# Loads issued a stage early, a third value buffer in GLA, its last head's end among its outputs, and a wait for constants moved, in a decoder layer on one Trainium2 core

## The reference

```python
mod = silu(c) @ w_ada + b_ada                      # shift1, scale1, gate1, shift2, scale2, gate2
h   = rmsnorm(x) * (1 + scale1) + shift1
p   = h @ w_in                                     # one projection for GLA, RWKV-7 and the two gates
# GLA, 4 heads: q, k of width 128, v and output gate of width 256, low-rank decay gate (rank 16)
la  = log_sigmoid(p_a @ w_gla_gate + b) / 16       # p_a: 16 columns of p, "gaT" in the kernel
per chunk of 64 tokens, with b = cumsum(la):
    o = (q exp(b)) S + tril((q exp(b)) (k exp(-b))^T) v
    S = exp(b_last) S + (k exp(b_last - b))^T v
og  = o * rsqrt(mean(o^2) + eps) * g * silu(gg)    # per head
# RWKV-7, 16 heads of 64: token shift, decay from a low-rank tanh, delta-rule state, group norm, gate
merged = sigmoid(g1) * (og @ w_b_gla) + sigmoid(g2) * (o_r @ w_b_rw)
x   = x + gate1 * rmsnorm(merged @ w_out)
# PEER: 8 heads, top-16 of 128 x 128 single-neuron experts, then gelu and a weighted sum
x   = x + gate2 * rmsnorm(peer(rmsnorm(x) * (1 + scale2) + shift2))
```

## Time and profile before

| | us |
|---|---|
| median of 3 runs | 5053.77 (5053.18 to 5062.45) |
| the profiled execution | 5051.28 |
| its span, first to last instruction | 5049.4 |
| mean granted TensorE clock | 0.922 |

### The profile page before, as it was taken

One profiled execution on the slowest core, in us unless ns is written; L12 is line 12 of the kernel. 1 busy time (PEld: TensorE's weight loads), 2 busy tenths in 40 slices (PEclk: granted clock), 3 DMA queues, 4 the chain that ended last, 5 costly groups with the idle time before them and its releaser, 6 DMA issues. The chain is left out here.

```text
span 5049.4 us, 80491 instructions
## 1 busy us (share of the span) xinstructions
PE 4346.1 (86%) x30920; PEld 2976.9 (59%) x30920; DVE 3328.2 (66%) x6528; ACT 1124.7 (22%) x2258; POOL 1677.7 (33%) x1412
## 2 busy tenths in 40 slices
PE   6999997875888887997988759999989899989970
PEld 6999996654777775653978634443434344434430
DVE  4232322445666661112997749999999999999998
ACT  2000001334555552124233320111100101111101
POOL 0000000001212210000143446666666566666666
PEclk9999998577999998998999879999999999999985
DMA  5422223211011014114022269999999999999987
GB/s 209 168 96 93 93 93 122 79 62 63 26 42 32 26 30 170 73 51 159 26 84 86 77 214 393 374 386 341 384 352 402 334 400 356 387 345 389 370 336 296
DMA packets 350603, 1012.43 MB, mean 201 GB/s; under 512 B 39116, under 2 KB 123020, under 8 KB 344760
## 3 DMA queue, kind: packets, MB, share of 16 engines
q0 software_dynamic: 156672, 570.49, 29.0%
q1 hardware_dynamic: 193592, 437.38, 23.9%
HBM read 903.76 MB, written 103.99 MB: 200 GB/s over the span
## 5 line engine op out<-in xcount | busy, mean ns | idle before, releaser
L2778 PE MATMUL peer_v_b<-peer_vt,peer_mix 128*128 128x512 f32 x2048 | 943.1, 615 | 123.8 <-DVE peer_mix L2615 80.0
L2766 PE MATMUL peer_s_b<-dense_hT_d,peer_ut 128*128 128x512 f32 x2048 | 901.0, 593 | 38.3 <-DMA peer_G2s<-mod 38.3
L2550 POOL DMA_INDIRECT peer_ring<-in_peer_v,peer_idx x544 | 712.6, 1310 | 290.1 <-issue 160.6
L2778 PEld LDWEIGHTS peer_v_b<-peer_vt,peer_mix 128*128 128x128 f32 x2048 | 402.0, 198 | 649.2 <-issue 495.9
L2544 POOL DMA_INDIRECT peer_ring<-in_peer_u,peer_idx x544 | 596.6, 1097 | 477.7 <-DVE peer_acc L2667 231.0
L2766 PEld LDWEIGHTS peer_s_b<-dense_hT_d,peer_ut 128*128 128x128 f32 x2048 | 389.7, 190 | 529.0 <-issue 490.4
L1524 POOL TENSOR_TENSOR rw_An<-rw_abT,rw_join 128x256 f32<-128x256 f32 x160 | 134.5, 847 | 1650.5 <-DVE rw_abT L1437 1316.2
L2667 DVE SCALAR_TENSOR_TENSOR peer_acc<-peer_ring,peer_coef,peer_acc 128x1024 f32<-128x1024 f32 x534 | 653.7, 1279 | 0.0
L2704 DVE CUSTOM_DVE_ANT_0 peer_ring<-peer_ring,peer_h 128x1024 f32<-128x1024 f32 x544 | 637.5, 1220 | 2.0 <-DVE peer_h L2681 1.0
L57 PE MATMUL proj_acc<-proj_hT_high,proj_w_low 128*128 128x352 f32 x1584 | 513.8, 324 | 16.7 <-DVEq L401 16.7
L58 PE MATMUL proj_acc<-proj_hT_low,proj_w_high 128*128 128x352 f32 x1584 | 508.6, 321 | 0.0
(11 more groups left out here) (424 smaller groups left out, 6531.6 us busy)
## 6 DMA issues: line engine op xcount, KB each, us to landing
peer_ut<-in_peer_ut SPq DMA_DIRECT2D x128, 512.0 KB, 8.1
peer_vt<-in_peer_v SPq DMA_DIRECT2D x128, 512.0 KB, 8.9
pT<-proj_o SPq DMA_DIRECT2D x66, 528.0 KB, 2.9
front_w<-in_w_in SPq DMA_DIRECT2D x66, 512.0 KB, 3.7
G<-route_G SPq DMA_DIRECT2D x32, 1024.0 KB, 9.3
peer_gt<-G SPq DMA_DIRECT2D x64, 512.0 KB, 7.2
proj_w_ada<-in_w_ada SPq DMA_DIRECT2D x16, 1024.0 KB, 6.1
peer_ring<-in_peer_u,peer_idx POOLq DMA_INDIRECT x544, 11.9
```

What stands on the lines that cost most here:

```text
L2550: pool.indirect_dma_start(out=ring[:, k, :], out_offset=None, in_=t["peer_v"], in_offset=bass.IndirectOffsetOnAxis(ap=idx[U % 2][:, k:k + ...
L2766: last = pe.matmul(s_b[:, n % 3, :], ut[:, n % UT, k, :], hT_d[:, k, :], start=(k == 0), stop=(k == KD - 1))
L2778: last = pe.matmul(v_b[:, m % 4, :], mix[:, part % 2, e, tokens], vt[:, part % 2, e, cols], start=(e == 0), stop=(e == PART - 1))
```

## The change

- `projection` takes a `GlaAhead` and an `RwkvConsts`. GlaAhead holds a room of 6 x M per partition, gaT, wz, cst and starts. The room's first part is the ring of `w_ada`, now of 3 chunks. Before the last two stores of pT, SP waits for the last chunk's use and for 13 stores of each buffer, and issues 9 loads for GLA (wz, cst, starts, q and k of head 0, values and gates of head 0) and the 13 constants of RWKV. The gate columns are copied straight into GLA's `gaT`; its DRAM tensor is gone, and the stores of `mod` no longer follow its store.
- `gla` has three value buffers (the first is the room's). `load_vg(2)` is issued after head 0's scaling, and in the loop the values of head h + 2 instead of h + 1.
- The last head follows a list of its own, in which its end (`l`) stands among its own turns, samples and outputs. GLA_ORDER serves the first three heads.
- `rwkv` finds its constants loaded. It puts its low-rank tiles into `bE` and `kE`, so the first pair's tiles are loaded at once, and stores the shift of the low-rank columns behind them. At pair 1 SP issues the loads of `MergeAhead`: ogT and both weights of the branches.
- `merge` loads only orT itself. Its two branches are two tiles, and the second block takes the first one's room.
- `peer_experts`: VectorE waits for `iota_in` at first and for `consts_in` only where tile 0 is finished; TensorE's wait for the constants is gone.
- `build` nests the stages so that what is shared lives long enough; this adds three clean-ups, one behind gla and two behind merge.

```diff
-def projection(nc, t, xT, modT, sg, w, w_in, wg, wg_in):
-    CHUNKS, RING, FIRST = 2 * KD, 4, 2
+def projection(nc, t, xT, modT, sg, w, w_in, wg, wg_in, ahead, consts):
+    CHUNKS, RING, FIRST = 2 * KD, 3, 2
-        wa = s.sb("w_ada", [P, RING, QUAD])
+        wa = ahead.room[:, :, :].rearrange("p a m -> p (a m)")[:, 0:RING * QUAD].rearrange("p (r c) -> p r c", r=RING)
-        og = s.sb("og", [16, M])
+        og = ahead.gaT
...
+                sp.wait_ge(wa_used, CHUNKS)
+                for n in range(W):
+                    sp.wait_ge(stored[n], 16 * (6 * GH // W + 1))
+                ahead.load(sp, t)
+                consts.load(sp, t)
                 for n in range(W):
                     sp.wait_ge(first_out, (ITER - 1) * W + n + 1)
                     sp.wait_ge(rest_out, (ITER - 1) * W + n + 1)
                     sp.dma_start(t["pT"][PT - W + n], o[:, n, :]).then_inc(stored[n], 16)
-                sp.wait_ge(first_out, PT + 1)
-                sp.wait_ge(rest_out, PT + 1)
-                sp.dma_start(t["gaT"], og[:, :]).then_inc(stored[0], 16)
...
 GLA_ORDER = (
     "eptepxspeetpopxxetespoxtsxepesoeteoxseptoxxpptsoepxtspxxoesppo",
 )
+GLA_LAST = (
+    "texeselllteoexexeteseoexetesexsotolxlstoxxtsoxtsxxolslollllll",
+)
...
-    for h in range(GH):
+    for h in range(GH - 1):
...
-    return steps + end(GH - 1)
+    return steps + last_head(GH - 1)
...
+class GlaAhead(Stage):
+    def load(self, sp, t):
+        sp.dma_start(self.wz[:, :, :], t["w_gate"].rearrange("h r p -> r h p")).then_inc(self.first_in, 16)
+        sp.dma_start(self.cst[:, :, :], t["gla_cst"].rearrange("h p n -> p h n")).then_inc(self.first_in, 16)
+        sp.dma_start(self.starts[:, :], t["starts"][:, 0:M].broadcast_to([P, M])).then_inc(self.first_in, 16)
+        for n in range(2):
+            sp.dma_start(self.room[:, n, :], t["pT"][n * GH]).then_inc(self.qk_in, 16)
+        for n in range(4):
+            sp.dma_start(self.room[:, 2 + n, :], t["pT"][2 * GH * (1 + n // 2) + n % 2]).then_inc(self.vg_in, 16)
...
-        vg = [s.sb(f"vg{n}", [P, 4, M]) for n in range(2)]
+        vg = [ahead.room[:, 2:6, :]] + [s.sb(f"vg{n}", [P, 4, M])[:, :, :] for n in (1, 2)]
...
                 sp.wait_ge(scaled, 3)
                 load_qk(1)
+                load_vg(2)
...
-                        if h + 1 < GH:
-                            load_vg(h + 1)
+                        if h + 2 < GH:
+                            load_vg(h + 2)
...
+class RwkvConsts(Stage):
+    def load(self, sp, t):
+        for name, shape in self.SHAPES.items():
+            dst = self.tiles[name]
+            src = t[name].broadcast_to([P, MW]) if name == "starts" else t[name]
+            sp.dma_start(dst[:, :, :] if len(shape) == 3 else dst[:, :], src).then_inc(self.consts_in, 16)
+class MergeAhead(Stage):
+    def load(self, sp, t):
+        sp.dma_start(self.gla[:, :, :].rearrange("p (h a) m -> p h a m", a=2),
+                     t["ogT"].rearrange("h p a m -> p h a m")).then_inc(self.gla_in, 16)
+        for n in range(2):
+            sp.dma_start(self.w[:, n, :, :, :], t["w_br"][n]).then_inc(self.w_in[n], 16)
...
                 for n in range(2):
-                    sp.dma_start(raw[n], t["pT"][RW0 + 24 + n]).then_inc(consts_in, 16)
-                sp.wait_ge(sho_ready, 1)
-                sp.dma_start(t["new_shift_wg"].rearrange("n p b -> p n b"), sho[:, 0:2, :]).then_inc(shift_stored, 16)
-                sp.wait_ge(wa_ready, 1)
-                sp.wait_ge(cleared, CLEARED)
+                    sp.dma_start(raw_wg[n], t["pT"][RW0 + 24 + n]).then_inc(consts_in, 16)
...
+                    if j == 1:
+                        ahead.load(sp, t)
...
-                sp.dma_start(r_.iota[:, :], t["iota"].broadcast_to([P, TOP])).then_inc(consts_in, 16)
+                sp.dma_start(r_.iota[:, :], t["iota"].broadcast_to([P, TOP])).then_inc(iota_in, 16)
...
-                dve.wait_ge(consts_in, 16 * CONSTS)
+                dve.wait_ge(iota_in, 16)
...
+                    if tile == 0:
+                        dve.wait_ge(consts_in, 16 * CONSTS)
...
-                pe.wait_ge(consts_in, 16 * CONSTS)
...
-    for stage in (front, gla, rwkv, merge, peer):
-        with nc.cleanup_on_exit():
-            stage(nc, t)
+    with nc.cleanup_on_exit(), ExitStack() as ctx:
+        consts = RwkvConsts(nc, ctx)
+        with nc.cleanup_on_exit(), ExitStack() as ctx1:
+            ahead = GlaAhead(nc, ctx1)
+            with nc.cleanup_on_exit():
+                front(nc, t, ahead, consts)
+            with nc.cleanup_on_exit():
+                gla(nc, t, ahead)
+        with nc.cleanup_on_exit(), ExitStack() as ctx2:
+            ahead = MergeAhead(nc, ctx2)
+            with nc.cleanup_on_exit():
+                rwkv(nc, t, consts, ahead)
+            with nc.cleanup_on_exit():
+                merge(nc, t, ahead)
+    with nc.cleanup_on_exit():
+        peer(nc, t)
```

More of the change, by code:

```diff
@@ L480, in _, with front @@
                 project(0, wg2, 16)
-def front(nc, t):
+def front(nc, t, ahead, consts):
     with ExitStack() as ctx:
@@ L500, in front @@
             modulation(nc, t, xT, modT, sg, first)
-        projection(nc, t, xT, modT, sg, w, w_in, wg, wg_in)
+        projection(nc, t, xT, modT, sg, w, w_in, wg, wg_in, ahead, consts)
 GH, GV, GC = 4, 256, 64
@@ L535, in gla_steps, with last_head @@
     relative = lambda which, h: [(kind, head - h, x) for kind, head, x in stream(which, h)]
+    def last_head(h):
+        streams = {which: iter(stream(which, h)) for which in "tsoxe"}
+        streams["l"] = iter(end(h))
+        return [next(streams[which]) for which in "".join(GLA_LAST)]
     whole = {which: iter(relative(which, 1)) for which in "tsoxpe"}
@@ L552, in gla @@
         seq_rows = s.sb("seq_rows", [NS, NB])
[L553 to L557, removed]
-        vg = [s.sb(f"vg{n}", [P, 4, M]) for n in range(2)]
+        starts, gaT, wz, cst = ahead.starts, ahead.gaT, ahead.wz, ahead.cst
+        qk = ahead.room[:, 0:2, :]
+        vg = [ahead.room[:, 2:6, :]] + [s.sb(f"vg{n}", [P, 4, M])[:, :, :] for n in (1, 2)]
         S_in = s.sb("S_in", [P, NB, GV])
@@ L1035, in rwkv @@
+def rwkv(nc, t, consts, ahead):
     with ExitStack() as ctx:
         s = Stage(nc, ctx, "rw")
-        ident = s.sb("ident", [P, RH])
-        strict = s.sb("strict", [P, 2, RC])
-        incl = s.sb("incl", [P, 2, RC])
-        first_l = s.sb("first_l", [P, RC])
-        first_u = s.sb("first_u", [P, RC])
-        join = s.sb("join", [P, LEVELS, RC])
-        seq_rows = s.sb("seq_rows", [P, NB])
-        starts = s.sb("starts", [P, MW])
-        heads = s.sb("heads", [P, P])
-        mean = s.sb("mean", [P, P])
@@ L1047, in rwkv @@
-        cst = s.sb("cst", [P, PAIRS, 10])
+        ident, strict, incl, first_l, first_u, join, seq_rows, starts, heads, mean, cst, mu_wg, sh_wg = (
+            consts.tiles[name] for name in consts.SHAPES)
         keep_k, keep_x = s.sb("keep_k", [P, PAIRS]), s.sb("keep_x", [P, PAIRS, 3])
-        mu_wg, sh_wg = s.sb("mu_wg", [P, 2]), s.sb("sh_wg", [P, 2, NB])
         sh = s.sb("sh", [P, 3, NB])
@@ L1246, in _ @@
                 for n in range(2):
-                    last = act.copy(sho[:, n, :], raw[n][:, SEQ - 1:M:NT])
+                    last = act.copy(sho[:, n, :], raw_wg[n][:, SEQ - 1:M:NT])
                 last.then_inc(sho_ready, 1)
@@ L1709, with merge @@
 MP = (TILES + 1) * P
-def merge(nc, t):
+def merge(nc, t, ahead):
     with ExitStack() as ctx:
         s = Stage(nc, ctx, "mg")
-        br = s.sb("br", [P, 2, KD, M])
+        br = [ahead.gla, s.sb("rw", [P, KD, M])]
         mT = s.sb("mT", [P, KD, M])
-        w = s.sb("w", [P, 2, 2, KD, P])
+        w = ahead.w
         gt = s.sb("gt", [P, 2, M])
@@ L2807, in scratch @@
 def scratch(nc, t):
-    for name, shape in {"mod": [NSEQ, 6, D], "pT": [66, P, M], "gaT": [16, M],
+    for name, shape in {"mod": [NSEQ, 6, D], "pT": [66, P, M],
                         "ogT": [GH, P, 2, M], "orT": [PAIRS, P, M],
```

108 lines of the change are left out of this document (54 added, 54 removed).

## The result

The changed kernel takes 4993.43 us (median of 4 runs, 4987.22 to 4997.36), against 5054.03 for the kernel before: a ratio of 0.989 with a 95% interval of 0.9876 to 0.9904, that is 48 to 63 us less. I had forecast 4980, a gain of 71.6 us; it came to about 60, with the time inside the range (4961 to 4998). On a second chip it took 4986.68 against 5049.31 (ratio 0.9878, 0.9862 to 0.9895). The profiled execution is the one of 4993.53 us, with a span of 4991.7.

What follows compares the result with a forecast made beforehand. Five stages run in sequence with no single bound; TensorE's waits at six places were to shrink. Gains of 9.9, 22.5, 2.0, 11.3, 15.1 and 13.2, less 2.4, make 71.6 us off 5051.3: forecast 4980, range 4961 to 4998 (8 in 10).

Steps and rivals of the forecast that it cites:

- term 3: GLA's last head, its end placed among its outputs: -11.3 us at the end, +9 inside the head, net -2 (ends -11, +5).
- rival B: Expert stage: saturated, it takes its gain of 13 us back, so an earlier start only queues; 4993 us, chance 0.13.
- Term 1: Projection to GLA: with loads ahead and gaT on chip, GLA starts at 848.5 instead of 858.4, -9.9 us.
- rival F: Projection: w_ada's ring of three lands chunks late and TensorE waits, up to +79 us, 5059, slower than before; chance 0.03.
- Term 2: GLA, heads 2 and 3: a third value buffer removes both stalls at the first transpose, -10.96 and -11.50, together -22.5 us.
- Rival E: GLA, heads 2 and 3: the stall is not the value load, or its load comes late; +22.5, 5002 us, chance 0.04.
- rival D: GLA's last head: its new order costs all that was bounded, net +5 us instead of -2; 4987 us, chance 0.10.
- Term 4: GLA to RWKV: constants loaded a stage early bring the scan to 22.1 us after RWKV's first instruction, from 33.4; -11.3 us.
- Term 5: RWKV to merge: operands loaded ahead in pair 1 let TensorE start at 1966.0 instead of 1981.11; -15.1 us.
- Term 6: Router to experts: TensorE starts when its first weights land, 2974.0, not at the last constant; -13.2 us (ends 0, -17).
- Term 7: Stage ends: one more clean-up behind GLA, two at merge's, at 0.8 us each; +2.4 us (ends 1 and 4).
- rival C: GLA: without the stalls, heads 2 and 3 begin at TensorE's full clock; 4965 us, chance 0.10.

## Why the prediction was right or wrong

The step that failed is term 3, the price of the last head's new order inside the head: +9 us forecast, +25.1 measured, so that the last head lost 12.5 us where a gain of 2 was forecast. The measured 4993 is also the price that I had put on rival B, whose mechanism did not occur, and it lies in the range only because B set its upper end; term 3 at its own worst (+5) gives 4987. That the range held is luck.

**Term 1, right.** 848.5 forecast, 847.91 measured. The ring of three cost nothing: rival F falls by the projection's unchanged waits.

**Term 2, right.** The values were the stalls; taking the early loads out brought back 9.9 and 11.0 us. Rival E falls.

**Term 3, wrong, and nearly all of the miss.** Its end was right (11.9 us forecast, 10.6 measured). Its body was not: I charged 9 us for the new order, 5 for TensorE's wait on the first square and 4 for two more sums of squares, and capped the net loss at +5. Measured are +25.1. The idle time of TensorE rose by 12.6 (13.7 for 1.2): the wait that I had walked, 6.05 for my 5, and 6.5 that I had not, 5.15 of it behind head 2's outputs on VectorE. I had followed ScalarE and TensorE through the list and left head 2's outputs in VectorE's queue out. Its busy time rose by 12.5: the two sums of squares took 2.72 and 2.63, 5.3 for my 4, and some 7 us remain, by subtraction, for a lower granted clock (0.66 for 0.80), which I had only as a word in the upper end. Against the old order in the same kernel, with heads 0 to 2 alike, it is 14.2 us of busy time (56.6 for 42.4), of which 9 remain (0.66 for 0.84). Removing the order, adding it alone and moving single steps all show it as the cause; how its waits and the clock hang together is seen only in that the clock rose whenever a wait went (0.66 to 0.70, 0.71 to 0.78). That is rival D's mechanism, which I held to 0.10 and priced at 4987, with a cost of 5 where 12.5 came.

**Term 4, right.** 21.4 us from RWKV's first instruction to the scan, 22.1 forecast. The two tiles landed at 4.7 instead of 6.1, and 0.9 of that was lost again: from landing to the tanh it took 6.7 us as before, where I had forecast 5.8.

**Term 5, right.** -15.2, and the cover held: TensorE goes from the first branch (16.55 us) to the second with no wait for orT, which lands 13.1 us after its issue, 3.5 ahead of its first use.

**Term 6, right.** -13.3, with the stage behind it unchanged: 2058.9 to 2061.5 us in all fourteen traces, with and without the wait. Rival B falls.

**Term 7, half.** Behind merge the two more cost 1.1 us together; behind GLA the one more cost nothing (4.17 and 4.19). 1.1 for 2.4.

**The clock, partly.** I gave the vanished stalls nothing, and with the stalls put back head 2 still took 59.3 us at 0.62; that bears the term out. The Trainium skill (TensorE: Matmul & The Clock Gate, "Why this matters for your kernels") has idle gaps between bursts of matmuls drop the engine to half clock. In the changed kernel's windows the clock fell in head 2 at about 1011 us:

```profile
1005.00:1010.00 5.00, 4.83 (x27) 3.41 (x26) 3.81 (x8) 4.08 (x7) 0.00 (x0) 1.00 0.00 0
1010.00:1015.00 5.00, 5.00 (x22) 4.37 (x21) 2.74 (x6) 2.61 (x5) 0.00 (x0) 0.57 0.00 0
```

from full clock (2.4 GHz) to half (1.2 GHz), with TensorE 0.17 us idle in the ten and no stall ahead in its head. The rule alone does not explain the clock of these heads, and rival C did not occur: head 2, with no stall ahead, ran its first 19 us at 0.50 with TensorE busy throughout, as head 1 had before:

```profile
974.41:993.40 18.99, 18.99 (x72) 14.70 (x72) 6.99 (x11) 9.59 (x13) 0.00 (x0) 0.50 0.64 250
```

But I took one execution's clock for a property of the code: head 0, wholly at half clock in the kernel before, took 52 to 54 us in every other trace, in one of them with the same code and the same wait ahead of it. The -10.2 of head 0 is such a chance. The +8.6 of head 2 (60.1 for 51.5) is one in so far as which head is long changes; but one of the three was long in nine of ten traces of the changed kernel's heads 0 to 2 with the loads early. Less its stalls the kernel before took 168.3 us for the three in one trace and 158.6 in the other, so that the missing stalls cost nothing on the average is not shown. In the measured execution the two entries nearly cancel, by luck.

## What to carry to other kernels

A list of steps that all engines walk must be followed through every engine's queue before it is priced: the step that hurts is one that stands in one engine's queue ahead of what another engine waits for. Here the end was hidden with profit where an engine had a block of its own work (the sigmoids under TensorE's 7 us of samples' matmuls), and at a loss ahead of it. Loads and waits between stages, by contrast (terms 1, 4, 5 and 6), came out within 1 us of the forecast, because the idle time and its releaser can be read straight from the timeline.

## What the runs showed of the hardware

The granted clock of TensorE differs from one execution to the next of the same code. With TensorE over 90% busy heads 0 to 2, stalls taken off, took 51 to 54 us at a mean of 0.63 to 0.76, 59 to 61 us at 0.61 or 0.62, or 63.9 at 0.50, and which of the three was the long one changed between executions of the same three heads. Their sum in the changed kernel's code with the loads early lay between 160.0 and 166.8 us, so a part of the scatter of 10 us between runs of this kernel can come from there; RWKV (780 to 786 us) and the router (606.5 to 611.7) vary too, with no change in their code. For a change of 10 us or less the same marks in several traces told more than the medians.
